# One block of a width-31 causal convolution on TensorE and three on VectorE, in place of two and two

## The chip, the cores and the metric

The kernel runs on one core of a Trainium2 chip. The metric is the device time of one execution in microseconds (us), as the median of several runs. The core's engines are TensorE (PE: matmuls, with weight loads PEld beside them), VectorE (DVE), ScalarE (ACT), GpSimd (POOL) and SyncE (SP), which here only issues DMAs. Each engine works through its own instructions in order and waits on semaphores for the others.

## What is computed

One layer of a hybrid decoder, for a prompt of 512 tokens and for 8 samples of 8 new tokens (576 columns in all), in 32-bit floats. The reference, cut to what matters here:

```python
proj = x @ p['w_in']
glu, qkv, og, beta_raw, dec_raw, g_a, g_b = jnp.split(proj, IN_OFFSETS, axis=-1)
glu = glu + p['b_glu']
u = glu[..., :CONV_CH] * jax.nn.sigmoid(glu[..., CONV_CH:])
cv, conv_new = causal_dwconv(conv_hist, u, p['w_dw'])      # width 31, 512 channels, one filter per channel
cv = jax.nn.silu(layer_norm(cv + p['b_dw'], p['ln_conv_g'], p['ln_conv_b']))
br_a = cv @ p['w_conv_out']
...
o, s_new = gated_delta_rule(q, k, v, beta, logdecay, s0)   # chunked, prompt in 4 tiles of 128 tokens here
o = o * lax.rsqrt(jnp.mean(o * o, -1, keepdims=True) + RMS_EPS) * p['dn_norm_g']
o = o * jax.nn.silu(og)
br_b = o @ p['w_dn_out']
mixed = jax.nn.sigmoid(g_a) * br_a + jax.nn.sigmoid(g_b) * br_b
h = layer_norm(DEEPNORM_ALPHA * x + mixed @ p['w_o'], p['ln1_g'], p['ln1_b'])
```

Cross-attention over a memory and a squared-ReLU MLP follow; the change doesn't touch them.

## The kernel before

Channels lie on the 128 partitions and tokens along the columns. Weights come in 152 chunks of 128x1024. Each chunk is loaded by SyncE (`load_w`, into two raw buffers), split by ScalarE into a high part (`w_hi`, line 1117) and by GpSimd into the rest (`w_lo`, line 493: it reads the raw chunk and `w_hi`, both in SBUF). A product is three matmuls per 128 rows of depth and per half of the columns (`gemm`, line 549): x_hi with w_hi, x_lo with w_hi, x_hi with w_lo. A chunk's slot in the ring of four is split anew when ScalarE has emptied the banks of the product that used it, so each finished product soon brings one GpSimd operation.

**The stage.** Between the q, k, v projection and the branch outputs lies the gated delta rule: a chain of small matmuls on TensorE with element-wise steps on VectorE and ScalarE between them. First come the samples' states, then the decays and products of the four heads, then a doubling inverse in six levels (`for n in range(len(NEAR))`), then a loop over the four prompt tiles, each with a new state `pst` (line 1929), and last the sums for the norms (`sum_rows`, line 670).

**The filler.** Between the steps of that chain each engine works off a common list, `ITEMS`, by calls of `between(n)`: TensorE in slices, four per item (`SLICES`). A gemm item is one chunk's product with x (`gate` and `glu` for u, `ga`, `gb`, `og` for the gates); its slice is 12 matmuls. A conv item is one block of 128 channels of the wide convolution. ScalarE and VectorE go through the same list and do an item's part in its fourth step: ScalarE the sigmoids of `gate`, `ga`, `og` and `gb` (line 1185) and the split of the chunk four further on, VectorE the write of `u` for `glu` (lines 1690 to 1693) and of `sgate` for `og` (line 1701). Items are numbered on from 12 (`item_place`). An item of even place uses banks 0 and 1, of odd place banks 2 and 3, and TensorE starts it when the item two places earlier has been emptied (`taken`). `REST` counts the slices that are left behind the last tile, before the sums for the norms; it is the number of slices of all items but `gb`, less the 63 used by then.

**The wide convolution** has four blocks of 128 channels, `CT`. The blocks in `PE_CONV` go to TensorE (`conv_taps` in its program, line 613): SyncE copies `u` of the block into `u4`, four times shifted, by 16 DMAs (`shifted`, line 415, which waits until VectorE has written that `u`), VectorE builds the stationary `wst` (`stationary`, line 1675), and 192 matmuls with 32 output rows each form the four slices. The other blocks go to VectorE tap by tap (`wide_taps`): one tap is an operation on the 512 prompt columns and one on the 64 sample columns, `cv = cv + w * u` (line 1620; the first tap of a block line 1618), with `u` and `cv` in SBUF. VectorE's `between(n, taps)` takes n steps of the list and then up to `taps` taps of the blocks whose `u` is written, in the order of the blocks. ScalarE squares `cv` (line 1297) for the norm when all taps are counted and the conv items emptied.

```python
for _ in range(REST - 2 * SLICES):
    between(1, 4)
wide_taps(len(todo), CT)
chc.wait()
for j in PE_CONV:
    dve.wait_ge(*emptied(("conv", j)))
```

These lines of VectorE's program (from 1933) stand behind the last tile. Of the 62 taps eight are left there; `REST` is 25.

Of the kernel before, what the change touches and what calls it, by code (L numbers as in the profile page):

```python
# [52 lines left out]
LATE = C_FF + KB  # L53
SLICES = 4
TAPS4 = (CONV_K + 3) // 4
PE_CONV = (2, 3)


GLU_ORDER = (2, 0, 3, 1)
ITEMS = [(k, i) for i in GLU_ORDER[:3] for k in ("gate", "glu")] + [("conv", 2), ("gate", 1), ("glu", 1), ("conv", 3)] \  # L60
    + [("ga", i) for i in range(KB)] + [("og", i) for i in range(CT)] + [("gb", i) for i in range(KB)]
USED = 32 + 2 * 3 + 1 + 2 * 5 + 2 + 3 * TILES
FILLED = len([i for i in ITEMS if i[0] != "gb"]) * SLICES
REST = FILLED - USED


# [5 lines left out]
def stored_at(c):  # L72

    if C_GLU <= c < C_GB:
        kind, i = [item for item in ITEMS if item[0] != "conv"][c - C_GLU]
        return {"gate": C_GLU + 2 * i, "glu": C_GLU + 2 * i + 1, "og": C_OG + i, "ga": C_GA + i}[kind]
    if C_GB <= c < C_AB:
        return C_GB + (c - C_GB if c < C_GB + 2 else 2 * (c - C_GB) - 1)
    if C_AB <= c < C_WO:
        return C_GB + (2 * (c - C_AB) + 2 if c < C_AB + 6 else c - C_GB)  # L80
    return c


def item_chunk(item):

    before = ITEMS[:ITEMS.index(item)]
    return C_GLU + len([i for i in before if i[0] != "conv"])
GROUPS, GT = DEC_BATCH // 4, 4 * DEC_SEQ


# [7 lines left out]
def build(nc, A):  # L98
# [190 lines left out]
    taken = [S("taken0"), S("taken1")]  # L289
# [91 lines left out]
    @block.sync  # L381
    def _(sp):
        def load_x(i):
            sp.dma_start(xraw[:, 2 * i:2 * i + 2], A["xT"][:, 2 * i:2 * i + 2]).then_inc(S(f"x_loaded{i}"), 16)

        def load_w(c):
            if c >= RAW:
                sp.wait_ge(lo_ready, c - RAW + 1)
            sp.dma_start(raw[:, c % RAW], A["w"][stored_at(c)]).then_inc(raw_loaded[c % RAW], 16)

        load_w(0)
        for i in range(4):
            load_x(i)
        load_w(1)
        sp.dma_start(wbd[:], A["wbd"][:]).then_inc(S("par_loaded"), 16)
        sp.dma_start(par[:], A["par"][:]).then_inc(S("par_loaded"), 16)
        sp.dma_start(qhist[:], A["qhist"][:]).then_inc(S("par_loaded"), 16)
        load_w(2)
        load_w(3)
        sp.dma_start(cst[:], A["cst"][:]).then_inc(S("cst_loaded"), 16)  # L400
        for e in range(2):
            rows = slice(e * BLK, (e + 1) * BLK)
            sp.dma_start(lmask[rows], A["lmask"][rows, 0:len(NEAR), rows]).then_inc(S("cst_loaded"), 16)
        for j in range(CT):
            sp.dma_start(u_s(j)[:, :, 0:CH], A["chist"][:, j]).then_inc(S("cst_loaded"), 16)

        def shifted(j):


            sp.wait_ge(*emptied(("glu", j)))  # L410
            if j > PE_CONV[0]:
                sp.wait_ge(S("conv_done"), j - PE_CONV[0])
            for t in range(4):
                for g in range(4):
                    sp.dma_start(u4[32 * t:32 * t + 32, g, 0:U4], u[32 * g:32 * g + 32, j, t:t + U4])\
                        .then_inc(S("u4_loaded"), 16)

        def weights(first, last):

            with sp.Fori(0, (last - first) // RING) as g:  # L420
                for s in range(RING):
                    chunk = sp.snap(g * RING + first + s)
                    used = sp.snap(g * RING + first + s - RAW + 1)
                    sp.wait_ge(lo_ready, used)
                    sp.dma_start(raw[:, s % RAW], A["w"][chunk]).then_inc(raw_loaded[s % RAW], 16)

        weights(4, C_GLU)
        for c in range(C_GLU, C_GLU + 4):
            load_w(c)
        for t in range(4):  # L430
            for g in range(4):
                a = PAR["w_dw"] + PE_CONV[0] * CONV_K + t
                n = len(PE_CONV) * CONV_K - t
                sp.dma_start(w4[32 * t:32 * t + 32, g, 0:n], A["par"][32 * g:32 * g + 32, a:a + n])\
                    .then_inc(S("u4_loaded"), 16)
        load_w(C_GLU + 4)
        load_w(C_GLU + 5)
        sp.wait_ge(S("qraw_free"), 1)
        for h in range(HEADS):
            sp.dma_start(sst[h][:], A["sdelta"][:, h]).then_inc(S("sst_loaded"), 16)  # L440
        sp.wait_ge(S("consts"), CONSTS)
        sp.wait_ge(S("cst_loaded"), 16 * (3 + CT))
        load_w(C_GLU + 6)
        shifted(2)
        for c in range(C_GLU + 7, C_GLU + 11):
            load_w(c)
        shifted(3)
        for c in range(C_GLU + 11, C_GB):
            load_w(c)
        for c in range(C_GB, C_WO):  # L450
            load_w(c)
        weights(C_WO, C_WO + 4)
        sp.wait_ge(gemm_done, C_WO)
        sp.dma_start(memraw[:], A["memT"][:]).then_inc(S("mem_loaded"), 16)
        weights(C_WO + 4, C_XQ + 4)
        sp.wait_ge(*ln("ln1", "res", KB, KB))
        for i in range(2 * DEC_BATCH):
            if i >= 4:
                sp.wait_ge(S("kv_used"), i - 3)
            sp.dma_start(kv[:, i % 4], A["v" if i // 4 % 2 else "kT"][i // 8 * 4 + i % 4])\  # L460
              .then_inc(S(f"kv_loaded{i % 4}"), 16)
            if i in (0, 2):
                weights(C_XQ + 4 + 2 * i, C_XQ + 8 + 2 * i)
        weights(C_XO + 4, CHUNKS)
        for i, part, what in ((2, LAST[0], "out"), (3, LAST[1], "aff")):
            for j in range(KB):
                sp.wait_ge(*at_part(what, i, j + 1))
                sp.dma_start(A["yT"][:, j, part], res[:, j, part]).then_inc(stored, 16)
        sp.wait_ge(stored, 16 * N_STORES)
        sp.wait_ge(S("states_out"), 16 * (HEADS - 1))  # L470
        sp.wait_ge(S("last_state_out"), 16)
# [66 lines left out]
    def _(pe):  # L538
# [89 lines left out]
        def filler():  # L628

            for item in ITEMS:  # L630
                kind, i = item
                o = item_place(item)
                if kind == "conv":
                    pe.wait_ge(S("u4_loaded"), 16 * 16 * (i - PE_CONV[0] + 2))
                    pe.wait_ge(S("wst_ready"), i - PE_CONV[0] + 1)
                else:
                    c = item_chunk(item)
                    pe.wait_ge(lo_ready, c + 1)
                pe.wait_ge(taken[o % 2], o // 2)
                for n in range(SLICES):  # L640
                    if kind == "conv":
                        ins = conv_slice(i, n, out_pair(o))
                        if n == SLICES - 1:
                            ins.then_inc(S("conv_done"), 1)
                    else:
                        ins = gemm(c % RING, out_pair(o), x, every[2 * n:2 * n + 2], opens=(n == 0), closes=(n == SLICES - 1))
                        if n == SLICES - 1:
                            ins.then_inc(gemm_done, 1)
                    yield
# [461 lines left out]
    def _(act):  # L1111
# [39 lines left out]
        def filler():  # L1151

            for item in ITEMS:
                kind, i = item
                o = item_place(item)
                for _ in range(SLICES - 1):
                    yield
                if kind == "conv":
# [439 lines left out]
    def _(dve):  # L1598
# [79 lines left out]
        def filler():  # L1678
            for item in ITEMS:
                kind, i = item  # L1680
                o = item_place(item)
                for _ in range(SLICES - 1):
                    yield
                if kind == "glu":
# [233 lines left out]
        for c in range(TILES):  # L1918
            for pr in range(2):
                dve.wait_ge(S("yz"), at_tile(c, pr))  # L1920
                V.tensor_tensor(ut[pr][:, c % 2], lines(ps[5 + 2 * pr][:, 0:2 * P], pr), bc(beta[:, c, 2 * pr:2 * pr + 2], P), mul)\
                    .then_inc(S("u_ready"), 1)
            between(1, 2)
            for pr in range(2):
                dve.wait_ge(S("ku"), at_tile(c, pr))
                dve.wait_ge(S("o_done"), at_tile(c, pr))
                for hh in range(2):
                    state = pst[:, 2 * pr + hh]
                    ins = V.scalar_tensor_tensor(state, state, eglast[:, 2 * pr + hh, c:c + 1], ps[4 + 2 * pr][:, hh * P:(hh + 1) * P],
                                                 mul, add)  # L1930
                ins.then_inc(S("s_new_p"), 1)
            between(2, 2)
        for _ in range(REST - 2 * SLICES):
            between(1, 4)
        wide_taps(len(todo), CT)
# [472 lines left out]
```

## Time and profile before

| | |
|---|---|
| median of 3 runs | 1209.33 us (1208.16 to 1210.84) |
| the profiled execution | 1205.99 us |
| its span, first to last instruction | 1204.2 us |
| mean granted TensorE clock | 0.982 of 2.4 GHz |
| TensorE busy | 1144.5 us |
| VectorE busy | 528.7 us |
| ScalarE busy | 426.4 us |
| GpSimd busy | 411.4 us |

The stage of the chain runs from about 105 to 430 us of the span. A row of a timeline gives the start and the length in us, the engine and the line, the operation, output<-inputs, shapes and how many instructions were merged; in brackets stands how long the engine was idle before, and what released it. A row of the stretches gives the stretch and its length, then the busy us of PE, PEld, DVE, ACT and POOL with their counts, the granted clock (1.00 is 2.4 GHz, 0.50 is 1.2 GHz), the DMA engines' share and GB/s.

### The profile page before, as it was taken

How to read it: one execution, taken by the hardware profiler on the slowest of the kernel's cores; microseconds unless marked ns; L12 is line 12 of the kernel's file. 1: busy time of each engine (PE TensorE's matmuls, PEld its weight loads, DVE VectorE, ACT ScalarE, POOL GpSimd, SP SyncE). 2: the span in 40 equal slices, each digit the busy share in tenths (PEclk: the TensorE clock that was granted, in tenths of full speed). 3: DMA queues.
4: the chain of work that ended last, by engine and by line, in shares of the span. 5: the costliest groups of instructions: out<-in, count | busy, mean ns of one | idle time of the engine just before them, and what ended most of it. 6: DMA issues, size and time to landing. Idle time of an engine off the chain costs nothing.

```text
span 1204.2 us, 22932 instructions
## 1 busy us (share of the span) xinstructions
PE 1144.5 (95%) x9645; PEld 1089.0 (90%) x9645; DVE 528.7 (44%) x977; ACT 426.4 (35%) x753; POOL 411.4 (34%) x206
## 2 busy tenths in 40 slices
PE   6999897799999899999899999999999999999996
PEld 6998787699898699999899659999999999999995
DVE  4786747884444543585600333633122112112237
ACT  5447112123223342233842332775133123213314
POOL 4343113001123133344654133656333333333302
PEclk9999999899999899999999999999999999999998
DMA  7224405001026122223465372224222222222102
GB/s 222 88 78 142 111 6 176 19 21 36 19 71 87 47 70 88 100 93 99 131 225 209 157 298 71 71 71 153 81 82 88 85 73 87 87 72 86 54 1 79
DMA packets 41602, 115.46 MB, mean 96 GB/s; under 512 B 14384, under 2 KB 16944, under 8 KB 39088
## 3 DMA queue, kind: packets, MB, share of 16 engines
q1 hardware_dynamic: 35632, 109.09, 27.9%
q10 hardware_dynamic: 5888, 5.18, 2.0%
q8 instruction: 63, 1.03, 0.3%
q14 instruction: 19, 0.16, 0.0%
HBM read 103.26 MB, written 7.53 MB: 92 GB/s over the span
## 4 chain that ended last, share of the span: by engine, by line
PE 50%; issue 27%; POOL 8%; DVE 2%; DMA 1%; ACT 1%; POOLq 0%; SPq 0%; ACTq 0%; DVEq 0%
PE bank L549 44%; POOL w_lo L493 8%; PE bank L982 1%; PE bank L965 1%; DMA kv<-v 1%; PE bank L1020 1%; PE bank L613 1%; PE bank L726 0%; PE bank L580 0%; ACT att_p L1430 0%; PE bank L1002 0%; PE bank L1028 0%; DVE sm L2103 0%; DVE att_p L2119 0%; PE bank L802 0%
## 5 line engine op out<-in xcount | busy, mean ns | idle before, releaser
L493 POOL TENSOR_TENSOR w_lo<-w_raw,w_hi 128x1024 fp32r<-128x1024 f32 x84 | 207.7, 2476 | 417.4 <-ACT w_hi L1117 417.2
L549 PE MATMUL bank<-x_hi,w_hi 128*128 128x288 f32 x640 | 197.4, 308 | 13.5 <-DVE x_lo L1603 8.6
L549 PE MATMUL bank<-x_lo,w_hi 128*128 128x288 f32 x640 | 191.9, 300 | 0.0
L549 PE MATMUL bank<-x_hi,w_lo 128*128 128x288 f32 x640 | 191.0, 298 | 0.0
L1117 ACT ACTIVATE w_hi<-w_raw 128x1024 fp32r<-128x1024 f32 x116 | 122.8, 1059 | 153.0 <-PE bank L549 112.2
L549 PEld LDWEIGHTS bank<-x_hi,w_hi 128*128 128x128 f32 x640 | 123.0, 192 | 21.5 <-issue 11.3
L549 PEld LDWEIGHTS bank<-x_hi,w_lo 128*128 128x128 f32 x640 | 123.5, 193 | 0.0
L549 PEld LDWEIGHTS bank<-x_lo,w_hi 128*128 128x128 f32 x640 | 123.4, 193 | 0.0
L529 POOL TENSOR_TENSOR w_lo<-w_raw,w_hi 128x1024 fp32r<-128x1024 f32 x28 | 67.1, 2398 | 101.4 <-ACT w_hi L1117 101.4
L529 POOL TENSOR_TENSOR w_lo_more<-w_raw,w_hi_more 128x1024 fp32r<-128x1024 f32 x28 | 67.1, 2397 | 100.6 <-ACT w_hi_more L1117 100.6
L549 PE MATMUL bank<-hid_hi,w_hi 128*128 128x288 f32 (+2 forms) x256 | 76.5, 299 | 0.0
L549 PE MATMUL bank<-hid_hi,w_hi_more 128*128 128x288 f32 (+2 forms) x256 | 76.3, 298 | 0.0
L549 PE MATMUL bank<-hid_lo,w_hi_more 128*128 128x288 f32 (+2 forms) x256 | 76.1, 297 | 0.0
L549 PE MATMUL bank<-hid_lo,w_hi 128*128 128x288 f32 (+2 forms) x256 | 76.1, 297 | 0.0
L549 PE MATMUL bank<-hid_hi,w_lo_more 128*128 128x288 f32 (+2 forms) x256 | 75.9, 297 | 0.0
L549 PE MATMUL bank<-hid_hi,w_lo 128*128 128x288 f32 (+2 forms) x256 | 75.9, 297 | 0.0
L2253 DVE TENSOR_TENSOR hs<-ht 128x576 f32<-128x576 f32 x24 | 18.2, 760 | 119.1 <-ACT ht L1562 119.1
L1117 ACT ACTIVATE w_hi_more<-w_raw 128x1024 fp32r<-128x1024 f32 x36 | 37.7, 1053 | 75.4 <-PE bank L549 64.1
L1620 DVE SCALAR_TENSOR_TENSOR cv<-u,par,cv 128x512 f32<-128x512 f32 x120 | 57.2, 541 | 0.1
L1562 ACT ACTIVATE ht<-bank 128x288 f32<-128x288 f32 x48 | 17.1, 408 | 100.0 <-PE bank L549 100.0
L2266 DVE TENSOR_TENSOR res<-res,bank 128x288 f32<-128x288 f32 x32 | 13.1, 451 | 86.0 <-PE bank L549 86.0
L1633 DVE SCALAR_TENSOR_TENSOR qkv<-qraw,par,qkv 128x512 f32<-128x512 f32 x36 | 44.1, 1225 | 14.4 <-ACT qkv L1145 14.3
(409 smaller groups left out, 3143.2 us busy)
## 6 DMA issues: line engine op xcount, KB each, us to landing
w_raw<-w SPq DMA_DIRECT2D x152, 512.0 KB, 3.5
kv<-kT SPq DMA_DIRECT2D x8, 1024.0 KB, 6.3
kv<-v SPq DMA_DIRECT2D x8, 1024.0 KB, 8.1
u<-u SPq DMA_DIRECT2D x32, 105.5 KB, 2.2
xraw<-xT SPq DMA_DIRECT2D x4, 576.0 KB, 6.1
sst<-sdelta SPq DMA_DIRECT2D x4, 512.0 KB, 5.3
sdelta_out<-sst ACTq DMA_DIRECT2D x4, 512.0 KB, 3.9
yT<-res SPq DMA_DIRECT2D x8, 192.0 KB, 1.9
```

Of the source, the lines that this page charges most:

```text
L493: nc.gpsimd.tensor_tensor(wlo[:, s], raw[:, s % RAW], whi[:, s].bitcast(f32), sub)\
L529: nc.gpsimd.tensor_tensor(w_lo(s), raw[:, s % RAW], w_hi(s).bitcast(f32), sub).then_inc(lo_ready, 1)
L549: ins = nc.tensor.matmul(bank[:, 0:b - a], lhsT=w[:, kb], rhs=cols_of(m, kb, a, b), start=(opens and i == 0 and j == 0), stop=(closes and ...
L613: ins = nc.tensor.matmul(at(bank[32 * g:32 * g + 32]), lhsT=wst[:, j % 2, g, q], rhs=src(u4[:, g], 4 * q), start=(q == 0), stop=(q == TAPS ...
L965: ins = nc.tensor.matmul(out_pair(mb)[0][:, 0:2 * P], lhsT=a[:, kb, mb * P:mb * P + P], rhs=w[:, s:s + 2, kb], start=(kb == 0 and j == 0), ...
L982: ins = T.matmul(ps[t // 2][:, (t % 2) * N_MEM:(t % 2 + 1) * N_MEM], lhsT=aq[:, 2 * h + d, t * P:(t + 1) * P], rhs=mk[:, 2 * h + d], start ...
L1117: A_(w_hi(slot_of(c)), raw[:, c % RAW], ACT.Copy).then_inc(hi_ready, 1)
L1562: ins = A_(ht[:, n % 2, half], out_pair(n)[h][:, 0:HALF], ACT.Relu)
L1620: ins = V.scalar_tensor_tensor(dst, src(k), w, dst, mul, add)
L1633: V.scalar_tensor_tensor(qkv[:, j, PT], qraw[:, j, k:k + SEQ], pc("w_short", j * SHORT_K + k), qkv[:, j, PT], mul, add).then_inc(S("q_conv ...
L2253: V.tensor_tensor(hs[:, n % 2], ht[:, n % 2], ht[:, n % 2], mul).then_inc(S("hid_sq"), 1)
L2266: ins = V.tensor_tensor(r, r, bank, add)
```

## The change

Block 2 of the wide convolution moves from TensorE to VectorE; block 3 stays. In the list the blocks' `gate` and `glu` come in the order 0, 3, 1, 2. The place of the first conv item is taken by an item `none`, which has no slices and passes its banks on by a count of VectorE; so the one conv item has place 19, between `glu` 1 and `gate` 2. `REST` becomes 21. VectorE's 93 taps are called four instead of two behind the new state of each tile.

```diff
-PE_CONV = (2, 3)
+PE_CONV = (3,)
...
-GLU_ORDER = (2, 0, 3, 1)
-ITEMS = [(k, i) for i in GLU_ORDER[:3] for k in ("gate", "glu")] + [("conv", 2), ("gate", 1), ("glu", 1), ("conv", 3)] \
+GLU_ORDER = (0, 3, 1, 2)
+ITEMS = [(k, i) for i in GLU_ORDER[:3] for k in ("gate", "glu")] + [("none", 0), ("conv", 3), ("gate", 2), ("glu", 2)] \
     + [("ga", i) for i in range(KB)] + [("og", i) for i in range(CT)] + [("gb", i) for i in range(KB)]
 USED = 32 + 2 * 3 + 1 + 2 * 5 + 2 + 3 * TILES
-FILLED = len([i for i in ITEMS if i[0] != "gb"]) * SLICES
+FILLED = len([i for i in ITEMS if i[0] not in ("gb", "none")]) * SLICES
 REST = FILLED - USED
@@ SyncE
         load_w(C_GLU + 6)
-        shifted(2)
-        for c in range(C_GLU + 7, C_GLU + 11):
-            load_w(c)
+        load_w(C_GLU + 7)
+        load_w(C_GLU + 8)
         shifted(3)
-        for c in range(C_GLU + 11, C_GB):
+        for c in range(C_GLU + 9, C_GB):
             load_w(c)
@@ TensorE and ScalarE, filler
+                if kind == "none":
+                    continue
@@ VectorE, filler
+                if kind == "none":
+                    dve.wait_ge(taken[o % 2], o // 2)
+                    V.engine_nop().then_inc(taken[o % 2], 1)
+                    continue
@@ VectorE, behind the new state of each tile
-            between(2, 2)
+            between(2, 4)
```

`stored_at` and `item_chunk` leave out `none` as they leave out `conv`, and the lines of the changed kernel stand up to seven further down. How the order moves at three places is shown by the programs' instructions (number, line, operation, shape, and the semaphores waited for).

TensorE at the first conv item (`u_72` is `u4`; L747 and L748 are the products with the samples' states), before:

```order
772 L747 MATMUL bank<-sst_115,skq 32x128 x8
773 L613 MATMUL bank<-u_72,wst 32x288 [waits taken0,wst_ready,u4_loaded]
774 L613 MATMUL bank<-u_72,wst 32x288 x15
775 L755 MATMUL bank<-cst,qkv 32x128 [waits s_z]
776 L756 MATMUL bank<-sks,pick 32x128
```

and now:

```order
772 L748 MATMUL bank<-sst_115,skq 32x128 x8
773 L612 MATMUL bank<-u_72,wst 32x288 [waits taken1,wst_ready,u4_loaded]
774 L612 MATMUL bank<-u_72,wst 32x288 x15
775 L756 MATMUL bank<-cst,qkv 32x128 [waits s_z]
776 L757 MATMUL bank<-sks,pick 32x128
```

The work stands at the same place; its wait is now on the banks of odd places (`taken1`) instead of the even ones.

VectorE ahead of the L2 norm's products (`w_75` is the taps' weights for `wst`), before:

```order
111 L1672 MEMSET w_75 32x8
112 L1675 TENSOR_TENSOR wst<-w_75,fold 128x1024 [waits dve_own]
113 L1675 TENSOR_TENSOR wst<-w_75,fold 128x1024
114 L1690 SCALAR_TENSOR_TENSOR u<-bank,par,sig 128x288 [waits gemm_done,taken0]
115 L1691 SCALAR_TENSOR_TENSOR u<-bank,par,sig 128x224
116 L1693 SCALAR_TENSOR_TENSOR u<-bank,par,sig 128x8x8
117 L1753 SCALAR_TENSOR_TENSOR qkv<-bank,qkv 128x288 [waits l2_bc,taken1]
```

and now:

```order
111 L1675 MEMSET w_75 32x8
112 L1678 TENSOR_TENSOR wst<-w_75,fold 128x1024 [waits dve_own]
113 L1697 SCALAR_TENSOR_TENSOR u<-bank,par,sig 128x288 [waits gemm_done,taken0]
114 L1698 SCALAR_TENSOR_TENSOR u<-bank,par,sig 128x224
115 L1700 SCALAR_TENSOR_TENSOR u<-bank,par,sig 128x8x8
116 L1621 TENSOR_SCALAR cv<-u,par 128x512 [waits taken1]
117 L1621 TENSOR_SCALAR cv<-u,par 128x64
118 L1760 SCALAR_TENSOR_TENSOR qkv<-bank,qkv 128x288 [waits l2_bc] x16
```

One `wst` is gone, and block 0's first tap stands behind the first write of `u`.

VectorE behind the last tile, from its new state to the reads of `og` 0 and 1, before (rows 383 to 396 are more taps):

```order
379 L1929 SCALAR_TENSOR_TENSOR pst<-pst,sm,bank 128x128 [waits o_done,ku]
380 L1929 SCALAR_TENSOR_TENSOR pst<-pst,sm,bank 128x128
381 L1620 SCALAR_TENSOR_TENSOR cv<-u,par,cv 128x512 [waits cv_taps]
382 L1620 SCALAR_TENSOR_TENSOR cv<-u,par,cv 128x64 [waits cv_taps]
...
397 L1701 TENSOR_TENSOR sgate<-bank,sig 128x288 [waits og_sig]
398 L1701 TENSOR_TENSOR sgate<-bank,sig 128x288
```

and now (rows 400 to 457 are more taps):

```order
394 L1936 SCALAR_TENSOR_TENSOR pst<-pst,sm,bank 128x128 [waits o_done,ku]
395 L1936 SCALAR_TENSOR_TENSOR pst<-pst,sm,bank 128x128
396 L1621 TENSOR_SCALAR cv<-u,par 128x512 [waits cv_taps]
397 L1621 TENSOR_SCALAR cv<-u,par 128x64 [waits cv_taps]
398 L1623 SCALAR_TENSOR_TENSOR cv<-u,par,cv 128x512 [waits cv_taps]
399 L1623 SCALAR_TENSOR_TENSOR cv<-u,par,cv 128x64 [waits cv_taps]
...
458 L1708 TENSOR_TENSOR sgate<-bank,sig 128x288 [waits og_sig]
459 L1708 TENSOR_TENSOR sgate<-bank,sig 128x288
```

Sixteen operations, eight taps, stood between the last state and the read of `og` 0; now 62 stand there, all 31 taps of block 2. In between, the groups of taps stand as before, but for one more tap ahead of the samples' decay products and the two more behind each of the first three tiles' states.

## Rows read from the trace of the kernel before

**Rows 1.** The page: busy time of each engine; the chain that ended last, by engine
```profile
PE 1144.5 (95%) x9645; PEld 1089.0 (90%) x9645; DVE 528.7 (44%) x977; ACT 426.4 (35%) x753; POOL 411.4 (34%) x206
...
PE 50%; issue 27%; POOL 8%; DVE 2%; DMA 1%; ACT 1%; POOLq 0%; SPq 0%; ACTq 0%; DVEq 0%
```

**Rows 2.** Busy us of each engine in two stretches, then granted clock, DMA share, GB/s
```profile
220.00:240.00 20.00, 12.94 (x320) 10.19 (x320) 17.59 (x35) 1.94 (x4) 0.00 (x0) 0.83 0.06 23
...
340.00:360.00 20.00, 20.00 (x152) 20.00 (x152) 7.74 (x14) 4.97 (x9) 7.76 (x3) 1.00 0.20 57
```

**Rows 3.** Timeline of TensorE: start, us, operation, idle before and its releaser
```profile
229.32 0.48 PE L834 MATMUL bank<-ident,bw 64*64 64x64 f32 x4 [7.06 <-DVE bw L1852]
...
399.72 0.84 PE L677 MATMUL bank<-nrm,cst 8*128 8x288 f32 x1 [6.01 <-DVE nrm L1965]
```

**Rows 4.** Timeline of ScalarE behind the last tile: where it waited for gemm items
```profile
341.24 0.71 ACT L1185 ACTIVATE sga<-bank 128x288 f32<-128x288 f32 x2 [2.81 <-PE bank L549]
...
366.84 0.71 ACT L1185 ACTIVATE sig<-bank 128x288 f32<-128x288 f32 x2 [4.74 <-PE bank L549]
...
379.63 0.41 ACT L1185 ACTIVATE sig<-bank 128x288 f32<-128x288 f32 x1 [4.74 <-PE bank L549]
```

**Rows 5.** Timeline of VectorE behind the last tile
```profile
338.63 9.11 DVE L1620 SCALAR_TENSOR_TENSOR cv<-u,par,cv 128x512 f32<-128x512 f32 x16
...
361.18 0.82 DVE L1701 TENSOR_TENSOR sgate<-bank,sig 128x288 f32<-128x288 f32 x2 [13.44 <-ACT sig L1185]
...
374.25 0.76 DVE L1959 TENSOR_TENSOR nrm<-nrm,cv_sq 128x576 f32<-128x576 f32 x1
```

**Rows 6.** Timeline of TensorE: the second conv item, slices 1, 3 and 4
```profile
214.59 2.15 PE L613 MATMUL bank<-u,wst 128*32 128x288 f32 x32
...
232.89 1.72 PE L613 MATMUL bank<-u,wst 128*32 128x224 f32 x32
...
236.57 2.61 PE L613 MATMUL bank<-u,wst 128*32 128x224 f32 x96
```

**Rows 7.** Timeline of VectorE and of TensorE near 123 us
```profile
121.09 2.36 DVE L1675 TENSOR_TENSOR wst<-w,fold 128x1024 f32<-128x1024 f32 x2
...
124.58 0.37 PE L549 MATMUL bank<-x_hi,w_hi 128*128 128x288 f32 x1 [2.10 <-DVE u L1693]
```

**Rows 8.** Timeline of TensorE and of VectorE at the first conv item
```profile
161.31 2.12 PE L613 MATMUL bank<-u,wst 128*32 128x288 f32 x32
...
161.56 0.69 DVE L1809 COPY sks<-bank 128x512 f32<-128x512 f32 x1 [1.98 <-PE bank L747]
...
162.95 0.28 DVE L1693 SCALAR_TENSOR_TENSOR u<-bank,par,sig 128x64 f32<-128x64 f32 x1
```

**Rows 9.** Timeline of SyncE's queue and of GpSimd near 135 us
```profile
124.46 10.46 SPq L415 DMA_DIRECT2D u<-u  x16
...
140.24 4.93 POOL L493 TENSOR_TENSOR w_lo<-w_raw,w_hi 128x1024 fp32r<-128x1024 f32 x2 [21.20 <-ACT w_hi L1117]
```

**Rows 10.** Timeline of VectorE in the second prompt tile
```profile
313.99 2.45 DVE L1620 SCALAR_TENSOR_TENSOR cv<-u,par,cv 128x512 f32<-128x512 f32 x4
...
319.82 0.42 DVE L1921 TENSOR_TENSOR ut<-bank,sm 128x256 f32<-128x256 f32 x1 [3.38 <-PE bank L891]
```

**Rows 11.** Timeline of VectorE: four taps with nothing beside them, and what follows
```profile
243.72 3.52 DVE L1620 SCALAR_TENSOR_TENSOR cv<-u,par,cv 128x512 f32<-128x512 f32 x8
...
247.15 0.69 DVE L1852 TENSOR_TENSOR bw<-near,lmask 128x512 f32<-128x512 f32 x1
```

**Rows 12.** Timeline of GpSimd behind the last tile
```profile
342.97 2.96 POOL L493 TENSOR_TENSOR w_lo<-w_raw,w_hi 128x1024 fp32r<-128x1024 f32 x1 [11.55 <-ACT w_hi L1117]
...
349.37 2.40 POOL L493 TENSOR_TENSOR w_lo<-w_raw,w_hi 128x1024 fp32r<-128x1024 f32 x1 [3.44 <-ACT w_hi L1117]
```

**Rows 13.** Stretches behind the two waits of rows 3, columns as in rows 2
```profile
232.00:236.00 4.00, 4.00 (x100) 3.21 (x98) 4.00 (x8) 0.27 (x1) 0.00 (x0) 0.90 0.01 4
...
404.00:408.00 4.00, 4.00 (x21) 4.00 (x22) 4.00 (x12) 0.00 (x0) 0.00 (x0) 0.64 0.00 0
```

More of the change, by code:

```diff
@@ L74, in stored_at @@
     if C_GLU <= c < C_GB:
-        kind, i = [item for item in ITEMS if item[0] != "conv"][c - C_GLU]
+        kind, i = [item for item in ITEMS if item[0] not in ("conv", "none")][c - C_GLU]
         return {"gate": C_GLU + 2 * i, "glu": C_GLU + 2 * i + 1, "og": C_OG + i, "ga": C_GA + i}[kind]
@@ L86, in item_chunk @@
     before = ITEMS[:ITEMS.index(item)]
-    return C_GLU + len([i for i in before if i[0] != "conv"])
+    return C_GLU + len([i for i in before if i[0] not in ("conv", "none")])
 GROUPS, GT = DEC_BATCH // 4, 4 * DEC_SEQ
@@ L1681, in filler @@
                 o = item_place(item)
+                if kind == "none":
+                    dve.wait_ge(taken[o % 2], o // 2)
+                    V.engine_nop().then_inc(taken[o % 2], 1)
+                    continue
                 for _ in range(SLICES - 1):
```

## The prediction

> **What bounds the kernel now.** I begin with busy time and the chain of the page [rows 1]. TensorE is busy 95% of the span, VectorE 44%, and TensorE leads the chain. Fewer TensorE instructions should therefore pay, unless the stage that loses them has another limit; what a stage waits for is read from the stage. The table by stretches [rows 2] shows two kinds. From 220 to 240 us VectorE is busy 17.59 of 20 us and TensorE 12.94: VectorE sets the pace. From 340 to 360 us TensorE is busy 20 of 20 us and VectorE 7.74. TensorE's waits say the same [rows 3]: 7.06 us for VectorE's `bw`, over at 229.32 us, and behind it no other until 6.01 us for `nrm`, over at 399.72 us. Between them TensorE is the bound and VectorE has room, but not at each moment.
>
> The stage that matters runs from the last prompt tile (about 339 us) to the sums for the norms. ScalarE's waits [rows 4] mark when gemm items end on TensorE: 366.84 (`og` 1) and 379.63 us (`og` 3), 12.79 us for two, so 6.40 us an item and 1.60 us a slice. VectorE [rows 5] runs its last eight taps from 338.63 us, idles 13.44 us, then from 361.18 us reads `og` 0 out of its banks. TensorE may start `og` 2 only when that read is done: there are two pairs of banks, taken in turn. Today this is never late.
>
> **What TensorE sheds.** The work list loses one conv item, four slices. The order of the list is otherwise such that slices 1 to 36 are of the same kinds as before; slices 37 to 40, before the second conv block, become `ga` 0. Their costs were [rows 6] 2.15, as much again for the second, 1.72 and 2.61 us: together 8.6, less about 0.1 each in which a slice's last matmuls overlap the next work, so 8.2 us of TensorE. What comes of it on the path:
> - slices 37 and 38 lie where VectorE sets the pace [rows 2, 3], so nothing;
> - slice 39 shrinks by 0.1, but TensorE then waits for `bw`, nothing; slice 40 by 2.6 − 1.6 = 1.0 us, and behind it TensorE is the bound: −1.0 us;
> - 21 slices stand behind the last tile in place of 25: 4 × 1.60 = −6.4 us, if VectorE keeps up.
>
> **What moves early on.** VectorE builds one `wst` instead of two [rows 7]: 2.36 / 2 = 1.2 us, just ahead of the `u` write for which TensorE waits 2.10 us. −1.2 us. The two taps that now stand early (one behind this write, one behind `s_gd`) are 0.7 and 0.9 us, on an engine that there waits for TensorE and for ScalarE: 0.
>
> The one conv item now has place 19, and so the banks of place 17, the last `glu` before it; before it had place 18, whose banks ScalarE had emptied long ago. TensorE starts it at 161.31 us without a wait, while VectorE only ends writing that `u` at 162.95 + 0.28 = 163.23 us [rows 8], because it stands behind the `sks` copy that waits for TensorE. New wait: 163.3 − 161.3 = +2.0 us; the products behind it are queued on TensorE and everything up to the state updates follows them. Bounds: 0, if the wait is taken back in the stretch where VectorE sets the pace, and 2.0; I take 2.0, since VectorE's chain there hangs on these products. The replaced `conv` item leaves a wait and a count on VectorE that are long met: 0.
>
> The SP queue issues its 16 copies into `u4` in 10.46 us [rows 9]. They now stand behind two more weight loads; the second waits for a GpSimd piece that ends near 140.24 + 4.93 / 2 = 142.7 us. So they are issued by 153.2 us, 8 us ahead of the conv item at 161.3: 0. What it costs if they come late is a rival below.
>
> Sum up to the last tile: −1.2 + 2.0 − 1.0 = −0.2 us.
>
> **Taps in the tiles.** Three times two more taps stand behind new states. Such a group runs [rows 10] 2.45 us from 313.99, and then VectorE idles 3.38 us for TensorE. Two taps more are 1.7 us: 0, with 1.7 us left.
>
> **Taps behind the last tile: the step that decides.** VectorE has 93 taps for 62; two are placed early, six in tiles, and 31 stand behind the last tile where 8 stood. All 31 come before the read of `og` 0. A tap is 247.15 − 243.72 = 3.43 us for four, 0.858 each [rows 11], so 26.6 us. But the eight taps of today took 9.11 us where 8 × 0.858 + 0.08 = 6.9 was due: 2.2 us more, with one GpSimd operation (342.97, 2.96 us long against 2.40 for the next) in their middle [rows 5, 12]. Each item that TensorE ends brings one such operation 1.7 us later (341.24, 342.97). In the new order `ga` 6, `ga` 7, `og` 0 and `og` 1 end at 341.0, 347.4, 353.8 and 360.2 us, so four fall into the run of taps: 4 × 2.2 = 8.8 us. Bounds: 0, if a tap and GpSimd don't hinder each other, and 4 × 2.4 = 9.6; I take 8.8, the only row of a tap under such an operation. The page "SBUF — State Buffer" of the Trainium skill, section "Who interferes with whom", says that a VectorE instruction with two SBUF inputs and a GpSimd one reading SBUF exclude each other for the whole instruction. By that rule the term would be the upper bound, 9.6, and the sum 0.8 higher; the lengthened GpSimd operation agrees with it.
>
> VectorE: 338.63 − 0.2 = 338.4, + 26.6 + 8.8 = 373.8, + 0.8 for the read of `og` 0 [rows 5] = 374.6 us. TensorE is ready for `og` 2 at 366.8 − 6.4 − 0.2 = 360.2. It waits 14.4 us. Then `og` 2 and `og` 3, 12.8 us: 387.4. After waits of 6 and 7 us TensorE's granted clock is at the lower level, 1.2 GHz, for a while: the stretch from 404 to 408 us is at 0.64 in the mean though work resumed at 399.72 us, that from 232 to 236 at 0.90 though it resumed at 229.32 [rows 3, 13]. That is about 7.1 and 3.5 us at half speed, of which half is lost: 1.7 to 3.6, I take 2.7. So 390.1 us, where before this work ended just ahead of 379.6.
>
> **The sum.** 390.1 − 379.6 = +10.5 us at the sums for the norms. What follows (6.0 us wait included) is in the same order and hangs on TensorE's arrival; VectorE's six adds for these sums (0.76 us each, the last at 374.25 us, [rows 5]) end near 375.4 + 4.6 = 380 us, or a few microseconds later where they wait for ScalarE's squares, which start when the taps end: covered by 390.1. The profiled execution takes 1205.99 us, so 1216.5; the median of the runs stands 3.3 above it, so 1209.3 + 10.4, about 1219.7 us.
>
> **The rivals.**
> (A) The forecast, 0.67: 1216 to 1224, as the port term and the clock fall.
> (B) GpSimd costs the taps nothing, or yields to them. Then 338.4 + 26.6 + 0.8 = 365.8, a wait of 5.6, + 12.8 + 2.7 = 381.3: +1.7, so 1211 us. For it: VectorE instructions that read PSUM run beside GpSimd unhindered. Against: the 9.11 us row. 0.12.
> (C) Faster: the run of taps is over before TensorE needs the banks, so that TensorE keeps all it sheds: −0.2 − 6.4 = −6.6, and −8.6 if the 2.0 us bank wait is taken back: 1201 to 1203 us. It decides at 360.2 us: VectorE would have to do 31 taps and a read in 21.8 us, 0.68 each. For it: VectorE is busy only 7.74 of 20 us there. Against: 0.858 is the pace of every undisturbed group. 0.08.
> (D) The `u4` copies land late, or the bank wait spreads into a second one: each microsecond late comes on top; 5 us late gives 1225. 0.08.
> (E) A smaller loss, one or two GpSimd operations falling beside the taps and a clock back at once: +4 to +6, 1213 to 1215. 0.05.
>
> **Chances.** A measurement of this kernel can tell about 0.2%, 2.4 us. Faster: (C), 0.08. Same: (B) for the larger part, 0.09. Slower: (A), (D), (E) and the rest of (B), 0.83. The range from 1211.5 to 1224 takes in the bounds of the port, clock and bank terms and most of (E), and leaves (C) and half of (B) and (D) out.
>
> **What would show it.** Right: TensorE waits some 14 us before `og` 2, ended by VectorE's `sgate`; the taps behind the last tile run about 35 us, with four of some 2.4 us or more; TensorE waits 2 us for `u` before the conv block; the low clock follows the long wait; GpSimd's operations there grow to near 3 us. Wrong: no wait before `og` 2, or one under 7 us; or a time that moved elsewhere, in the tiles or before 240 us.

## The result, and the profile after

| | before | after |
|---|---|---|
| median | 1208.74 us (1207.49 to 1210.84, 4 runs) | 1220.55 us (1219.75 to 1225.6, 4 runs) |
| ratio, 95% interval | | 1.01 [1.0081, 1.0119] |
| profiled execution, its span | 1205.99, 1204.2 us | 1221.35, 1219.4 us |
| mean granted clock | 0.982 | 0.973 |

The changed kernel is slower, by 10 to 14 us by that interval; 1219.7 was forecast. In the 46 runs that went with the experiments the kernel before had medians of 1209.5 and 1209.7 us; against those the loss is about 11 us.

The page of the changed kernel, part 1, to be held against [rows 1]. TensorE lost 4.0 us of busy time and 192 matmuls, VectorE gained 31.8 us. That is less than the 8.2 us of work that TensorE was to shed, and the clock has the rest: it worked 34.9 us at the lower level, where it was 26.7 before, and half of the difference, 4.1 us, is lost:
```profile
PE 1140.5 (94%) x9453; PEld 1085.1 (89%) x9453; DVE 560.5 (46%) x1038; ACT 425.5 (35%) x751; POOL 412.8 (34%) x206
```
So TensorE does less, and the time is longer. The waits say where. These are TensorE's waits from 340 to 420 us, as totals with their count and the longest. The kernel before had one wait there, of 6.01 us for `nrm` [rows 3]:
```profile
PE bank L548 <- DVE sgate L1708: 14.2, 1, 14.2
PE bank L678 <- DVE nrm L1972: 6.0, 1, 6.0
```
The timeline of TensorE (start, us, operation, idle time before it and what ended it) where each wait ends:
```profile
163.50 0.89 PE L612 MATMUL bank<-u,wst 128*32 128x288 f32 x9 [1.88 <-DVE u L1700]
...
375.02 0.58 PE L548 MATMUL bank<-x_hi,w_hi 128*128 128x288 f32 x1 [14.17 <-DVE sgate L1708]
```
VectorE's timeline behind the last tile, to be held against [rows 5]. The new state `pst` ends the tile, then 31 taps run as one block, and only then are `og` 0 and `og` 1 read out:
```profile
338.56 0.60 DVE L1936 SCALAR_TENSOR_TENSOR pst<-pst,sm,bank 128x128 f32<-128x128 f32 x2 [0.73 <-PE bank L905]
339.08 0.77 DVE L1621 TENSOR_SCALAR cv<-u,par 128x512 f32<-128x512 f32 x2
339.76 34.38 DVE L1623 SCALAR_TENSOR_TENSOR cv<-u,par,cv 128x512 f32<-128x512 f32 x60
374.06 1.54 DVE L1708 TENSOR_TENSOR sgate<-bank,sig 128x288 f32<-128x288 f32 x4
```
GpSimd's timeline there, to be held against [rows 12]: four operations fall under the taps (2.79, 2.83, 2.88 and 2.86 us), and the next one, with no taps beside it, takes 2.40:
```profile
343.42 2.79 POOL L492 TENSOR_TENSOR w_lo<-w_raw,w_hi 128x1024 fp32r<-128x1024 f32 x1 [11.11 <-ACT w_hi L1118]
...
362.62 2.86 POOL L492 TENSOR_TENSOR w_lo<-w_raw,w_hi 128x1024 fp32r<-128x1024 f32 x1 [3.52 <-ACT w_hi L1118]
384.87 2.40 POOL L492 TENSOR_TENSOR w_lo<-w_raw,w_hi 128x1024 fp32r<-128x1024 f32 x1 [19.40 <-ACT w_hi L1118]
```
Taken one by one, the taps show where the time goes. The first of these GpSimd operations lasts from 343.42 to 346.21 us, and one VectorE operation, the 64-column part of a tap, lasts almost as long:
```profile
343.86 2.44 DVE L1623 SCALAR_TENSOR_TENSOR cv<-u,par,cv 128x64 f32<-128x64 f32 x1
```
The same operation takes 0.27 to 0.28 us where nothing is beside it. It ends 0.1 us behind the GpSimd operation, and under each of the other three GpSimd operations one such operation takes 2.36 to 2.43 us. So each GpSimd operation holds up one VectorE operation, by 2.1 us, and the rest of the taps run at their usual pace.
ScalarE's timeline, to be held against [rows 4]. `og` 1 ends on TensorE at 360.88 us, 6.0 us earlier than before; `og` 3 at 389.54, 9.9 us later:
```profile
360.88 0.71 ACT L1188 ACTIVATE sig<-bank 128x288 f32<-128x288 f32 x2 [4.74 <-PE bank L548]
...
383.14 0.71 ACT L1188 ACTIVATE sig<-bank 128x288 f32<-128x288 f32 x2 [4.27 <-PE bank L548]
...
389.54 0.41 ACT L1188 ACTIVATE sig<-bank 128x288 f32<-128x288 f32 x1 [4.74 <-PE bank L548]
```
Busy us of each engine by stretches, then granted clock (the columns of [rows 2]); the first is the counterpart of the second row there. VectorE went from 7.74 to 20 us of 20, and TensorE does 5.83 us of work in the next 20:
```profile
340.00:360.00 20.00, 20.00 (x152) 20.00 (x151) 20.00 (x33) 4.98 (x9) 8.50 (x3) 1.00 0.17 54
360.00:380.00 20.00, 5.83 (x33) 5.62 (x32) 19.86 (x39) 6.36 (x11) 2.86 (x1) 0.66 0.17 53
...
375.00:379.00 4.00, 3.98 (x19) 4.00 (x20) 3.90 (x7) 3.87 (x7) 0.00 (x0) 0.59 0.00 0
...
413.00:419.00 6.00, 6.00 (x24) 5.25 (x23) 5.14 (x15) 0.00 (x0) 0.00 (x0) 0.50 0.00 0
```
The last two rows are TensorE behind its two waits: it is at work, and mostly or wholly at the lower level of its clock, 1.2 GHz.

Matmul by matmul against before, the changed kernel is 0.45 us late all through the tiles, 9.9 us at the end of `og` 3, and 11.0 us once the clock is back at 419 us. It stays between 8.9 and 11.1 up to 719 us. The profiled execution ends 14.6 us late: at 731 us TensorE waits 2.83 us for `kv`, where it was 1.67, and has 6.8 us of low clock there. Profiles of the kernels below show this wait at 1.7 or near 2.6 us whatever their edit, so it isn't put down to the change.

### The profile page after: what moved, and what is told of

The parts are those of the page before. It is cut to its first block, busy times and chain, and to the rows that moved or that the text cites. A ratio compares the mean times of both kernels' runs of the same rounds, so it can differ in the third digit from the quotient of the medians.

```text
span 1219.4 us, 22589 instructions
## 1 busy us (share of the span) xinstructions
PE 1140.5 (94%) x9453; PEld 1085.1 (89%) x9453; DVE 560.5 (46%) x1038; ACT 425.5 (35%) x751; POOL 412.8 (34%) x206
## 4 chain that ended last, share of the span: by engine, by line
PE 49%; issue 27%; POOL 8%; DVE 3%; DMA 1%; ACT 0%; POOLq 0%; SPq 0%; ACTq 0%; DVEq 0%
PE bank L548 43%; POOL w_lo L492 8%; PE bank L983 1%; PE bank L1021 1%; DMA kv<-v 1%; PE bank L612 1%; PE bank L966 0%; DVE cv L1623 0%; PE bank L727 0%; PE bank L579 0%; ACT att_p L1433 0%; PE bank L1003 0%; PE bank L1029 0%; DVE sm L2110 0%; DVE att_p L2126 0%
## 5 line engine op out<-in xcount | busy, mean ns | idle before, releaser
L548 PE MATMUL bank<-x_hi,w_hi 128*128 128x288 f32 x640 | 198.9, 311 | 27.7 <-DVE sgate L1708 14.2
L1623 DVE SCALAR_TENSOR_TENSOR cv<-u,par,cv 128x512 f32<-128x512 f32 (+1 forms) x180 | 94.9, 594 | 0.2
```

What stands on the lines that cost most here:

```text
L548: ins = nc.tensor.matmul(bank[:, 0:b - a], lhsT=w[:, kb], rhs=cols_of(m, kb, a, b), start=(opens and i == 0 and j == 0), stop=(closes and ...
L1623: ins = V.scalar_tensor_tensor(dst, src(k), w, dst, mul, add)
```

## The experiments

All are edits of the changed kernel but the last. In the same runs the kernel before had medians of 1209.71 us (21 runs, first four experiments) and 1209.51 us (25 runs, last four).

**GpSimd away from the taps.** The low parts of the four weight chunks that fall under the taps are filled with zeros by GpSimd in place of a subtraction that reads two tiles from SBUF; these low parts are left out of the result.
```
-        lo_parts(C_GLU + 8, C_XO + RING)
+        lo_parts(C_GLU + 8, C_OG + 8)
+        for c in range(C_OG + 8, C_OG + 16):
+            pool.wait_ge(hi_ready, c + 1)
+            if C_OG + 10 <= c < C_OG + 14:
+                nc.gpsimd.memset(wlo[:, c % RING].bitcast(f32), 0.0).then_inc(lo_ready, 1)
+            else:
...
```


> The changed kernel, but GpSimd's four operations that fall beside the taps behind the last tile (the low parts of the chunks of og 2, og 3, gb 0 and gb 1) are replaced by writes of zeros that read nothing; these low parts are left out of the products. If it is GpSimd's reads that lengthen the run of taps (theory), the run shrinks from 35.1 to 26.6 us, TensorE's wait for sgate from 14.2 to about 5.7 us, and the time falls by 8 to 10 us against the changed kernel. If the run is long for another reason (DMA traffic, ScalarE, the taps themselves), the run stays near 35 us and the time within 1 us of the changed kernel. If GpSimd's operation as such is in the way, reading or not, the same: 35 us.

Measured: 1211.1 us (1208.78 to 1216.55, 10 runs), ratio to before 1.0021 [1.0006, 1.0035]. The timeline of VectorE, then of GpSimd:
```profile
339.76 25.86 DVE L1630 SCALAR_TENSOR_TENSOR cv<-u,par,cv 128x512 f32<-128x512 f32 x60
365.52 1.55 DVE L1715 TENSOR_TENSOR sgate<-bank,sig 128x288 f32<-128x288 f32 x4
```
```profile
343.40 0.95 POOL L507 MEMSET w_lo<- 128x1024 f32 x1 [11.09 <-ACT w_hi L1125]
```
The same taps take 25.86 us, not 34.38: 8.5 us for four operations, 2.1 each. TensorE's wait before `og` 2 is 5.65 us, not 14.17. GpSimd is still busy under the taps, for 0.95 us four times, and costs them nothing. So it isn't GpSimd's being active that costs. Nor is it only that the fills are shorter: the tap operation that starts at 343.86 us takes its usual 0.28 us and ends while the first fill (343.40 to 344.35 us) still runs. What this run doesn't separate is the reading of SBUF from the subtraction that went with it.

**Two more taps a group in the tiles undone.**
```
-            between(2, 4)
+            between(2, 2)
```


> The changed kernel with two taps instead of four behind each tile's state, so that 37 instead of 31 taps stand behind the last tile. If the run of taps ahead of the read of og 0 sets the time (theory), each tap more costs its 0.86 us: +5.2 us against the changed kernel, TensorE's wait 19.3 us instead of 14.2, and nothing gained in the tiles. If the taps in the tiles are in TensorE's way (rival), the tiles get shorter and the time rises by less than 3 us.

Measured: 1223.22 us (1221.78 to 1227.18, 4 runs), ratio 1.0123 [1.0104, 1.0142]. TensorE waits 16.75 us, 2.6 more:
```profile
377.83 0.58 PE L548 MATMUL bank<-x_hi,w_hi 128*128 128x288 f32 x1 [16.75 <-DVE sgate L1708]
```
The number was missed because the count of taps was: 34 of the 37 come before the read of `og` 0, three between it and the next. Three taps more before the read cost 2.6 us, 0.86 each, as an undisturbed tap [rows 11]. So the wait is made of taps, one for one, and six taps in the tiles are free (VectorE there still idles 0.20 to 2.31 us after them in the changed kernel). The rise of 2.67 us is also within what the rival allowed, but its cause is not there: from the first tile's `ut` to the last new state it is 41.59 us here (295.86 to 337.45) and in the changed kernel (295.63 to 337.22), so the tiles got no shorter.

**Taps on both sides of the reads.** Two taps a step behind the last tile in place of four, so that 20 precede the read of `og` 0, eight the next, three follow.
```
-            between(1, 4)
+            between(1, 2)
```


> The changed kernel with two instead of four taps per step of the list behind the last tile: 20 taps, the read of og 0, eight, the read of og 1, three; the same work in another order. If it is the order of these reads behind the taps that costs (theory), TensorE's wait of 14.2 us becomes two of about 3 us each, and the sums for the norms start near 380 us instead of 389.5: -8 to -10 us against the changed kernel, about as fast as the kernel before. If VectorE's sum of work is the limit whatever its order (rival), TensorE waits as long at the sums for the norms, and the time changes by less than 3 us.

Measured: 1212.9 us (1210.77 to 1216.7, 6 runs), ratio 1.0033 [1.0018, 1.0048]. TensorE's waits behind 340 us:
```profile
PE bank L678 <- DVE nrm L1972: 8.2, 1, 8.2
PE bank L548 <- DVE sgate L1708: 3.6, 2, 2.6
```
The same 31 taps are done, on the same engine and in the same stretch, and 7.7 us come back, because 14.2 us of waiting become 3.6 in two waits. That is just short of the 8 to 10 us that were expected, and one wait takes the place of another. The last taps now end near 378 us, and everything that hangs on them moves: ScalarE's squares, and behind them its reads and splits for `og` 2 and `og` 3, which now follow each other closely. And just ahead of its part of the norms ScalarE waits 2.08 us for a weight chunk, as it doesn't in the changed kernel:
```profile
397.52 1.06 ACT L1118 ACTIVATE w_hi<-w_raw 128x1024 fp32r<-128x1024 f32 x1 [2.08 <-DMA w_raw<-w]
```
TensorE waits 8.2 us for `nrm` instead of 6.0.

**Ten taps ahead of the tiles.**
```
-        between(3, 2)
+        between(3, 12)
         for c in range(TILES):
```


> The changed kernel with ten more taps ahead of the first tile, where VectorE idles 10.07 us; 21 instead of 31 stay behind the last tile. Theory: the ten fit into the idle time for nothing, the run behind the last tile becomes 18.0 us for the taps and 6.5 to 8.6 for three or four GpSimd operations, TensorE's wait 3.7 to 5.8 us; against the changed kernel -9 to -12 us, so between 2 us faster than the kernel before and equal to it. Rival: the added taps delay the first tile (its chain would start later than 295.63 us), and less than 8 us come back.

Measured: 1212.43 us (1208.29 to 1216.69, 10 runs), ratio 1.002 [1.0004, 1.0035]. The timeline of VectorE and of TensorE:
```profile
341.21 26.66 DVE L1623 SCALAR_TENSOR_TENSOR cv<-u,par,cv 128x512 f32<-128x512 f32 x42
```
```profile
368.75 0.58 PE L548 MATMUL bank<-x_hi,w_hi 128*128 128x288 f32 x1 [5.77 <-DVE sgate L1708]
```
21 taps and four GpSimd operations: 21 × 0.858 + 4 × 2.15 = 26.6. Ten taps fewer shorten the wait by 8.4 us. The gain on the changed kernel is 8.1 us, a little less than the 9 to 12 that were expected. The added taps don't delay the first tile: ahead of its `ut`, at 297.76 us, VectorE still waits 1.48 us for TensorE, and the run with taps on both sides of the reads, which moves none there, reaches it at 298.56.

**The conv item on the even place.**
```
-... + [("none", 0), ("conv", 3), ("gate", 2), ("glu", 2)] \
+... + [("conv", 3), ("none", 0), ("gate", 2), ("glu", 2)] \
```


> The changed kernel with the conv item on the even place 18, whose banks ScalarE emptied long before, and the empty place behind it. Theory: TensorE's 1.9 us wait for u at 163.5 us is gone, and the products behind it start earlier; because VectorE sets the pace between 200 and 230 us, where the shift of the changed kernel was already down to about 0.5 us, between 0.4 and 1.9 us of it remain: 1218.7 to 1220.2 us against 1220.55, the long wait before og 2 unchanged near 14 us. Rival (it is all taken back in the stretch that VectorE paces): 1220.5, no change. Rival (the wait moves to another operation, the u4 copies): a wait of over 1 us stays between 161 and 165 us.

Measured: 1220.56 us (1219.1 to 1222.22, 5 runs), ratio 1.0089 [1.0074, 1.0104]: no change against 1220.55. The wait for `u` before the conv item is gone from the trace. Yet from the end of the first wait for `u` to the end of the wait for `bw` it is 105.49 us here (126.85 to 232.34) and 105.48 in the changed kernel (124.15 to 229.63). So the time is the first rival's, but not its cause. Counted from that first wait, VectorE's `su` comes 2.1 us earlier here than in the changed kernel. Then 1.66 us are lost where this profile has a low clock from 176.7 to 180.1 us that the other lacks (VectorE waits 7.10 us for TensorE there instead of 5.43), and 0.43 at 215 us, in another wait for TensorE at its lower level (0.65 us instead of 0.22). Whether the even place is worth anything without such a stretch, this profile can't tell.

**Nineteen taps ahead.** The ten above, five more ahead of `su`, four ahead of the first new state of the samples; 12 stay behind the last tile.
```
         decay_rows(1)
-        between(2)
+        between(2, 5)
...
-        between(3)
+        between(3, 6)
         dve.wait_ge(S("s_yz"), 1)
```


> The changed kernel with 19 of the 31 last taps moved ahead: ten behind the last step before the tile loop, as in the run before, five behind the samples' between-steps ahead of su (where VectorE idles 6.0 us) and four ahead of the first new state (where it idles some 5 us). 12 taps stay behind the last tile: 12 x 0.86 + 2 or 3 GpSimd operations x 2.1 + 0.8 = 16 us from 339, so the first read ends near 355, before TensorE wants the banks at 360. Theory: no wait before og 2, the 6.4 us of the shed item are kept, only the usual clock loss behind the wait for nrm; 1209.3 - 6.4 + 0.4 = 1203 us, 1202 to 1206 if the moved taps delay an early step by up to 2 us. Rival (taps placed early delay VectorE where TensorE waits for it, between 200 and 230 us): each microsecond comes on top, 1208 to 1212. Rival (a lost wait is made up elsewhere by the clock): the time is as the kernel before, 1209, with a lower granted clock somewhere between 360 and 400 us.

Measured: 1205.7 us (1204.07 to 1210.27, 9 runs), ratio 0.9975 [0.9961, 0.9989]. There is one wait of TensorE left behind 340 us, `nrm`. VectorE now waits for `og` 0:
```profile
341.52 14.69 DVE L1623 SCALAR_TENSOR_TENSOR cv<-u,par,cv 128x512 f32<-128x512 f32 x24
357.67 0.82 DVE L1708 TENSOR_TENSOR sgate<-bank,sig 128x288 f32<-128x288 f32 x2 [1.46 <-ACT sig L1188]
...
365.60 2.86 DVE L1959 TENSOR_TENSOR nrm<-nrm,cv 128x576 f32<-128x576 f32 x1
```
The first result is the theory's: with no wait before `og` 2 the kernel is faster than before. The last row shows the GpSimd term on another instruction: under a GpSimd operation this addition takes 2.86 us, and the next of its kind, with none beside it, 0.76. The stage gained what was expected: the wait for `nrm` ends at 396.21 us, where it ends at 402.24 in the control below, 6.0 us later. The median gained 3 us on that control instead of 6. Between the two profiled executions the gain is 6.4 us when TensorE takes up `kv` at 716.8 us and 3.2 at its last sum: it waits 2.65 us for `kv` against 1.67, and has 6.8 us of low clock there against none. Why that wait has two lengths was not tried.

**Nineteen ahead, and the even place.** Both edits together.


> Both edits: 19 taps ahead and the conv item on the even place. Theory: the sum of the two effects, 0 to 2 us under the kernel with 19 taps ahead alone: 1201 to 1204 us, no wait of over 1 us at 161 to 165 us and none before og 2, faster than both the kernel before and the changed one. Rival (the even place gives nothing, since VectorE sets the pace later): the same time as with the 19 taps alone.

Measured: 1203.76 us (1199.47 to 1207.29, 12 runs), ratio 0.9951 [0.9936, 0.9966]. It beats both kernels: the one before by 5.8 us, or 4 to 8 by the interval, the changed one by 17. What the even place adds here isn't settled: 1.9 us in the medians, with intervals that overlap, and none in the experiment alone. TensorE's waits from 340 to 420 us:
```profile
PE bank L678 <- DVE nrm L1972: 6.0, 1, 6.0
```

**Control: the kernel before with its last eight taps ahead of the tiles.** The same edit as for ten ahead, in the kernel before.


> Control: the kernel before (two blocks on TensorE, 62 taps) with the same step before its tile loop doing up to ten more taps, so that its last eight taps move ahead of the tiles. Theory: the taps behind the last tile were never waited for there (VectorE read og 0 in time), so 0: 1209 us, at most 1 us more if the ten taps delay the first tile. Rival (placing taps there costs by itself, which would explain why ten ahead did not bring the changed kernel below 1209): 2 us or more slower.

Measured: 1208.65 us (1205.72 to 1212.44, 12 runs), ratio 0.9996 [0.9983, 1.0009]. Placing taps there costs nothing, and taking them from behind the last tile brings nothing where nobody waited for them. So it isn't the place of the ten taps that keeps the kernel with ten ahead above 1209 us. What that kernel still has is the wait of 5.77 us and, behind it, 5 us of work at the lower level of the clock.

## Why the prediction was right

- **The bound, and where.** The kernel got slower though its bounding engine sheds work, by a VectorE read for which TensorE waits: the wait is 14.17 us, and 14.4 was forecast. Every experiment that shortens this wait gives the time back.
- **The taps.** 26.6 + 8.8 = 35.4 us were forecast and 35.06 measured. With GpSimd's reads away the 31 run from 339.08 to 365.62, 26.5 us; four GpSimd operations add 8.5, 2.1 each, where 2.2 was taken. The Trainium skill's page "SBUF — State Buffer" has the rule that was weighed, in its sections "SBUF: two separate sides" and "Who interferes with whom": a VectorE instruction with two SBUF inputs and a GpSimd instruction that reads SBUF exclude each other, and the one that started first holds the other off until it is done. The trace agrees with it: the held operation (343.86 to 346.30 us) ends with the GpSimd operation, and the GpSimd operation, which starts under an operation of a tap, grows by 0.4 us. The term by it would have been 9.6, 1.1 too much, since what VectorE loses is 2.44 less the 0.28 that its operation takes anyway, and not GpSimd's whole 2.40. The second section also says that a GpSimd instruction that only writes SBUF does not contend with such a VectorE one; the 0.95 us fills beside undisturbed taps agree with it.
- **The six taps in the tiles** cost nothing, as forecast, but with some luck: 1.7 us were to be left. In the third tile a GpSimd operation (329.50 us, 2.81 long) fell beside the four taps, which took 5.63 us, and 0.20 us of VectorE's idle time was left. The sum had no such operation there.
- **The stages ahead.** −0.2 us was forecast at the last tile, +0.45 measured. All three terms of that sum were off, and that they nearly cancel is luck. Building one `wst` less brought 0.4 us at 124 us and not 1.2, since the copy into `pick` ahead of it took 0.91 us in this run and 0.11 before. The bank wait came as 1.88 of 2.0 us, and the conv item started 2.2 us late (163.50 for 161.31), but at 229.63 us only 0.3 was left [rows 3]. It wasn't taken back by VectorE's pace. About 0.5 us went at 194 us, where ScalarE waited 0.41 us for a weight chunk before and doesn't now. 1.15 went at 212 us, in a wait of VectorE for TensorE (the two rows below, before and after): TensorE was at its lower level until 212.3 us before, and only until 211.0 now. The −1.0 us of slice 40 was cancelled by the clock too: behind the wait for `bw` TensorE works 5.3 us at its lower level (to 234.9 us), where it was 3.5 (to 232.8), 0.9 us lost.
```profile
212.00 1.13 DVE L1820 SCALAR_TENSOR_TENSOR decay<-bank,sm,not_yet 128x128 f32<-128x128 f32 x4 [1.36 <-PE bank L778]
...
212.52 1.13 DVE L1827 SCALAR_TENSOR_TENSOR decay<-bank,sm,not_yet 128x128 f32<-128x128 f32 x4 [0.22 <-PE bank L779]
```
- **The clock.** 2.7 us was taken for the loss behind the long wait. TensorE resumed at 375.02 and had its clock back at 378.3, so 3.3 us at half speed, 1.6 lost. The rest came one wait later, where the sum had it at nothing: behind `nrm` TensorE ran low for 9.6 us (409.62 to 419.25) and did so for 7.1 before (399.72 to 406.86), 1.2 lost. That the two together come near the forecast's 2.7 is luck. So the work was 9.9 us late at `og` 3, where 10.5 was forecast, and 11.0 behind the norms.
- **The other cases.** (B), that GpSimd costs the taps nothing, gives 1211 us; the experiment that makes it true gives 1211.1. (C), that TensorE keeps all it sheds, needed the taps to be over by 360 us; with 12 left there, they are. (D) did not come: the `u4` copies were issued by 153.7 us. (E) needed one or two GpSimd operations beside the taps, and four came.

## What to carry over

When work moves from the bounding engine to an idle one, ask not how busy the receiver is but when its next result is wanted and what is queued ahead of it: 31 taps of 0.86 us on an engine that was busy 39% of that stretch cost 14 us, and the same taps, 19 of them moved into earlier gaps, cost nothing. Price the receiver's instructions with what runs beside them: taps with two SBUF operands lost 2.1 us to each GpSimd operation of 2.40 us that reads SBUF. And a wait of the bounding engine costs more than its length: behind the one of 14.17 us TensorE worked 3.3 us at half speed before its clock was back.

## What was not expected of the hardware

The clock behind two waits of TensorE is not a function of the wait's length. After 14.17 us of idle time it worked for 3.3 us at the lower level. Then it worked 28.6 us, waited 6.01 us, and was at the lower level for 9.6 us of work. In the run without GpSimd's reads, after 29.4 us of work and the same wait, it was 7.2 us. In the profiled runs the stretch behind the `nrm` wait that was at the lower level lasted 10.2 or 13.7 us in all, counted from its fall, though the wait was 6.0 us in nearly all of them.
